# The last feed-forward of a three-layer block: the second tile's down product one turn later, and a score product of the attention one block earlier

## The reference

```python
def conv_ffn(h, w_up, conv_w, conv_b, w_down):
    a, g = jnp.split(h @ w_up, 2, axis=-1)
    return (a * jax.nn.gelu(dwconv_centred(g, conv_w, conv_b), approximate=False)) @ w_down
```

## Time and profile before

| | before |
|---|---|
| median of three runs | 1090.57 us (1090.29 to 1094.52) |
| the profiled execution | 1090.13 us |
| its span, first to last instruction | 1088.3 us |
| TensorE matmul busy | 1060.3 us |
| VectorE, ScalarE busy | 791.5 us, 548.8 us |
| mean granted TensorE clock | 0.994 of full |
| DMA traffic | 232.91 MB |

### The profile page before, as it was taken

One profiled execution on the slowest core, in us unless ns is written; L12 is line 12 of the kernel. 1 busy time (PEld: TensorE's weight loads), 2 busy tenths in 40 slices (PEclk: granted clock), 3 DMA queues, 4 the chain that ended last, 5 costly groups with the idle time before them and its releaser, 6 DMA issues. The chain is left out here.

```text
span 1088.3 us, 20414 instructions
## 1 busy us (share of the span) xinstructions
PE 1060.3 (97%) x8020; PEld 966.8 (89%) x8020; DVE 791.5 (73%) x1374; ACT 548.8 (50%) x934; POOL 112.0 (10%) x133
## 2 busy tenths in 40 slices
PE   6999999999999999999999999999999998999998
PEld 1889778999999989888999999888866898999998
DVE  2688785787888778846677775797349767777776
ACT  4642485544444474655444444446347664444442
POOL 2102004000000027510000000300330010000000
PEclk9999999999999999999999999999999999999999
DMA  9981375698988716475787785396630144545541
GB/s 363 411 316 42 114 242 166 259 351 325 354 324 337 288 59 243 164 268 203 268 284 270 265 290 199 106 326 203 134 78 28 40 156 155 193 162 195 169 169 39
DMA packets 68594, 232.91 MB, mean 214 GB/s; under 512 B 12144, under 2 KB 12432, under 8 KB 68144
## 3 DMA queue, kind: packets, MB, share of 16 engines
q1 hardware_dynamic: 62496, 227.27, 58.9%
q0 software_dynamic: 5888, 3.73, 1.6%
q10 hardware_dynamic: 144, 1.05, 0.3%
HBM read 230.91 MB, written 1.05 MB: 213 GB/s over the span
## 5 line engine op out<-in xcount | busy, mean ns | idle before, releaser
L1757 PE MATMUL bank<-h_hi,w_hi 128*128 128x256 f32 (+2 forms) x1424 | 409.4, 288 | 4.7 <-DVE h_lo L1709 1.7
L1759 PE MATMUL bank<-h_hi,w_lo 128*128 128x256 f32 (+2 forms) x1424 | 406.0, 285 | 0.0
L1758 PE MATMUL bank<-h_lo,w_hi 128*128 128x256 f32 (+2 forms) x1424 | 405.3, 285 | 0.0
L1114 DVE TENSOR_TENSOR w_lo<-w_raw,w_hi 128x1024 fp32r<-128x1024 f32 x271 | 328.5, 1233 | 71.8 <-ACT w_hi L674 70.5
L674 ACT CAST w_hi<-w_raw 128x1024 fp32r<-128x1024 f32 x271 | 276.5, 1046 | 79.8 <-PE bank L1759 70.3
L1757 PEld LDWEIGHTS bank<-h_hi,w_hi 128*128 128x128 f32 x1424 | 269.4, 189 | 13.8 <-issue 7.3
L1758 PEld LDWEIGHTS bank<-h_lo,w_hi 128*128 128x128 f32 x1424 | 269.8, 189 | 1.6 <-issue 0.2
L1759 PEld LDWEIGHTS bank<-h_hi,w_lo 128*128 128x128 f32 x1424 | 269.8, 189 | 1.4
L1757 PE MATMUL bank<-g_hi,w_hi 128*128 128x256 f32 x544 | 155.4, 286 | 4.2 <-DVE g_lo L1374 2.5
L1758 PE MATMUL bank<-g_lo,w_hi 128*128 128x256 f32 x544 | 153.8, 283 | 0.0
L1759 PE MATMUL bank<-g_hi,w_lo 128*128 128x256 f32 x544 | 153.6, 282 | 0.0
(11 more groups left out here) (181 smaller groups left out, 1243.2 us busy)
## 6 DMA issues: line engine op xcount, KB each, us to landing
w_raw<-weights SPq DMA_DIRECT2D x281, 512.0 KB, 4.9
a_raw<-ada SPq DMA_DIRECT2D x140, 512.0 KB, 5.4
vals<-ada SPq DMA_DIRECT2D x4, 512.0 KB, 8.7
a_raw<-rpb POOLq DMA_DIRECT2D x9, 224.0 KB, 16.8
bias<-rpb POOLq DMA_DIRECT2D x7, 224.0 KB, 8.4
xT<-xt SPq DMA_DIRECT2D x1, 1024.0 KB, 9.4
big<-ctx SPq DMA_DIRECT2D x1, 1024.0 KB, 14.1
big<-ctx ACTq DMA_DIRECT2D x1, 1024.0 KB, 6.5
```

The source lines that it names most:

```text
L1114: nc.vector.tensor_tensor(w_lo[:, s, :], w_raw[:, s, :], w_hi[:, s, :].bitcast(fp), SUB)\
L1757: nc.tensor.matmul(out, a_hi, b_hi, start=start, stop=False)
L1758: nc.tensor.matmul(out, a_hi, b_lo, start=False, stop=False)
L1759: return nc.tensor.matmul(out, a_lo, b_hi, start=False, stop=stop)
```

## The change

In the last feed-forward `down(1)` of turn t is taken out of turn t and done in turn t + 1, between `up(0)` and `up(1)` (`down_before`). Turn 0 has five blocks, turns 1 to 10 have six, and turn 10 does its own `down(1)` at the end besides. The weights lie in memory in that order, so the splits of turn i are of blocks 3 to 8 counted from its start instead of 4 to 9. The sixth block (`W_FF2 + 5`) is split ahead of the feed-forward by both engines: by ScalarE before the root of norm 7, by VectorE before the inverse. `hi(6)` and `lo(6)` fall away in turn 0 and are there in turn 10. The waits of `normed` on `w_used` are counted anew.

In the attention, score pair 1 stands before value block 23 instead of after it, and the wait for the last turned queries stands before score pair 2.

```diff
@@ ScalarE, before the root of norm 7; VectorE, before invert(("norm", 7))
-                    split_to(W_FF2 + LEAD)
+                    split_to(W_FF2 + 5)
@@ ScalarE and VectorE, hi(j) and lo(j) of ffn
+                        if layer == 2:
+                            j -= 1
...
-                    hi(5)
+                    hi(5, layer < 2 or i)
...
-                    hi(6, splits_on)
+                    hi(6, splits_on and (layer < 2 or i) or layer == 2 and i == FT // 2 - 1)
@@ VectorE, normed
-                        dve.wait_ge(w_used, 6 * i + (w0 + 2 * s + e + 1))
+                        dve.wait_ge(w_used, 6 * i + (w0 + 3 * s + e + (first and s == 0)))
@@ VectorE, turn
-                    lo(5)
+                    lo(5, layer < 2 or not first)
...
-                    lo(6, splits_on)
+                    lo(6, splits_on and not (layer == 2 and first) or layer == 2 and final)
@@ TensorE, attention
-                        if name == "mla" and j == 0:
-                            pe.wait_ge(head_ready, MLA_H)
+                        if j == 0:
+                            pe.wait_ge(head_ready, MLA_H if name == "mla" else MLA_H + UNITS)
@@ TensorE, ffn
+                    def down_before():
+                        pe.wait_ge(split_done, 6 * i + splits_to(w0 + 1))
+                        pe.wait_ge(ff_lo, 2 * i + g0)
+                        for j in range(KT):
+                            a = wtile(w0 + 1, j * P, P)
+                            ins = split3(bank[tiles[("acc", layer, j // 2)][0]][:, (j % 2) * T:(j % 2 + 1) * T], a[0], a[1],
+                                         g_hi[:, 1, :], g_lo[:, 1, :], False, False)
+                        ins.then_inc(w_used, 1)
...
                     up(0)
+                    if layer == 2 and not (isinstance(i, int) and i == 0):
+                        down_before()
                     up(1)
                     last = isinstance(i, int) and i == FT // 2 - 1
-                    for s in range(2):
+                    for s in range(2 if layer < 2 or last else 1):
@@ TensorE, values of the attention
-                if s == 22:
+                if s >= 22:
                     pe.wait_ge(head_ready, MLA_H + 10)
-                    scores("na", head_rows, 0)
+                    scores("na", head_rows, s - 22)
...
-            pe.wait_ge(head_ready, MLA_H + UNITS)
-            attention("na", NA_H, 16, head_rows, lambda h, kt: vals[:, kt, h * NA_D:(h + 1) * NA_D], 12, 1)
+            attention("na", NA_H, 16, head_rows, lambda h, kt: vals[:, kt, h * NA_D:(h + 1) * NA_D], 12, 2)
@@ pack_weights
+        if at == W_FF2:
+            n = np.arange(3 * FT).reshape(FT // 2, 6)
+            order = [n[0, :5]] + [np.r_[n[t, 0:2], n[t - 1, 5], n[t, 2:5]] for t in range(1, FT // 2)] + [n[-1, 5:]]
+            w[at:at + 3 * FT] = w[at:at + 3 * FT][np.concatenate(order)]
```

More of the change, by code:

```diff
@@ L1329, in turn @@
                 def turn(i, splits_on=True, more=True):
+                    first, final = (isinstance(i, int) and i == n for n in (0, FT // 2 - 1))
                     def lo(j, on=True):
+                        if layer == 2:
+                            j -= 1
                         if on:
@@ L1381, in turn @@
                         norm_gain(5)
-                    lo(4, layer < 2 or not isinstance(i, int) or i)
-                    lo(5)
+                    lo(4, layer < 2 or not first)
+                    lo(5, layer < 2 or not first)
                     if sums > 1:
@@ L1997, in up @@
                         ws = [w0 + 2 * s + e for e in range(2)]
+                        if layer == 2 and not (isinstance(i, int) and i == 0):
+                            ws = [w0 - 1 + 3 * s + e for e in range(2)]
                         if layer == 2:
```

## The result

The changed kernel took 1085.47 us, the median of five runs (1082.91 to 1086.01). The kernel before, beside it, took 1093.55 (1090.29 to 1094.52): a ratio of 0.9923, interval 0.9897 to 0.9949. With more runs on another chip it was 1084.89 against 1093.81, a ratio of 0.9908 (0.9885 to 0.9931). So it is faster by 8 to 9 us. The forecast was 1081.0, range 1079.0 to 1084.7: the measured time lies 0.8 us above the range. The first profiles show neither plainly. Their spans are 1088.3 and 1083.7 us, 4.6 apart.

The account below looks back on a forecast made before the run. TensorE, busy for 97% of the span, was taken as the bound; 1.25 + 2.63 + 1.56 + 2.8 + 1.0 = 9.2 us off 1090.13 gives 1080.9, put at 1081.0, range 1079 to 1084.7.

Parts of the forecast that it names:

- the level: Whole kernel: 9.2 us off the profiled 1090.13 gives 1080.9; the runs' median is 0.44 higher, so 1081.0.
- The rule of the Trainium skill: Clock gate: slow matmuls differ from run to run; turn 0's half clock might be luck, the sum 1.56 us smaller.
- Turn 0 and the turns after it: Last feed-forward: turn 0 gains 1.25 us at `down(0)`, 2.63 at `down(1)`, 1.56 by the clock; turns 1 to 9, 2.8.
- The price of the clock: Half-clock stretch after turn 0's pauses, expected not to come once they are gone: 1.56 us gained.
- The account of turn 0: Turn 0's chain to `down(0)` is late behind two VectorE splits; with both gone from there, `down(0)` gains 1.25 us.
- The cover of a steady turn: Steady turn: `convolve(0)` starts 2.2 us late, its chain ends at 10.9, wanted at 14.4: 3.5 us in hand.
- Rival C: VectorE falls behind, `down(0)` stalls in all ten turns: 1096; chance 0.04 including the bank rule beside it.
- The attention: Start of the attention: second waiting transpose at 810.0 instead of 811.05, 1.0 us gained; bounds 1.7 and nothing.
- A: Half clock comes elsewhere, or `down(0)` of turn 0 still waits up to 1.3 us: 1082.4 to 1083.7; chance 0.14.
- B: Turn 0 is not mended, its loss having another cause; 2.8 + 1.0 us are left: 1086.3; chance 0.09.
- D: The moved product waits for something new in order, say its block's split; 3.9 us in hand; counted within B.
- the swing of the clock beside C: Going round PSUM banks idles TensorE between groups, the clock swings: 1.56 us a turn, net 1097; 1 in 100.

Follow-up runs that it names:

- fillers in turn 0: Kernel before with two filler matmuls on TensorE between `down(0)` and `down(1)` of turn 0: 1093.51 us against 1093.58, ratio 0.9994.
- the early split alone: Kernel before with the sixth block split ahead of the feed-forward and nothing moved: 1090.62 us against 1093.58, ratio 0.9971.
- changed and timed: The changed kernel once more, timed beside the kernel before in more rounds; its trace took 798.8 us to score pair 0 and 286.0 from there.
- three added operations: Changed kernel with three more split-sized VectorE operations ahead of the first gate tile in turns 1 to 10: feed-forward 238.47 us, period 19.62.

## Why the prediction was wrong in its number and right in most of its steps

**The step that failed is the last one, the level.** I set the sum against one execution of 1090.13 us and put the median 0.44 above it. The four times in view were 1090.13, 1090.29, 1090.57 and 1094.52, and I took the last for a stray. With 24 runs the kernel before has a median of 1093.58 (1088.03 to 1096.89): 1090.13 was a quick execution. Its trace has none of the costly stretches near 186, 398 and 472 us and a mean granted clock of 0.994; of the 24 runs the five at 0.994 or more took 1088.0 to 1092.4 us, the eight at 0.989 or less 1093.4 to 1096.9. 1093.6 less 9.2 is 1084.4; with that step mended the number would have been a microsecond off. The range had room for errors in the gain and none for the level, which alone spreads by several microseconds.

**The rule of the Trainium skill** was weighed in the prediction only against turn 0's stretch, and that was the wrong place for it. At turn 0 the stretch came in each of the three traces that keep the old feed-forward whole, with 12 slow matmuls in one and 15 and 16 in the others, and its removal paid 1.5 us. At the places of the unchanged part, which the prediction didn't look at, it comes in some traces and not in others. The page TensorE: Matmul & The Clock Gate (part 1, on the HAM clock gate) has the number of slow matmuls change from run to run of one kernel. The traces agree.

**Turn 0 and the turns after it**: forecast 1.25 + 2.63 + 1.56 + 2.8 = 8.24 us, measured 8.5. `down(0)` 1.25; the two down products of turn 0 took 10.00 us before and 5.68 now, 4.32 (forecast 4.19; I left out the first matmul after a wait, after which the next starts 0.20 us on instead of 0.12); nine turns at 0.32. The price of the clock, 1.56 in the forecast, was 1.58 against the kernel with fillers in turn 0.

**The account of turn 0** was right in naming the splits ahead of the chain. It gave the whole gain to the change as one; the early split alone carries 3.55 us of it.

**The cover of a steady turn** held, but with less in hand than I wrote. `g_lo` of s = 0 was forecast for 10.9 in the turn and ended at 10.8, the tile of s = 1 for 17.4 and 17.3; these positions were good. The 3.5 us derived from them was not: it is 1.0. Rival C would have begun there already, and its chance was drawn too small for the reason given. That this did no harm here is the luck of a margin that was a third of what I thought.

**The attention**: forecast 1.0 us. It arrived (1.06 us at the first weighing) and half of it was given back: from there to the output projection TensorE needs 48.5 us instead of 48.0, in three steps of 0.15 to 0.19, each at the second transpose of a pair; only the last, at 835.25, has a listed wait, for ScalarE's copy. What holds the other two stays open. The bound "nothing if the later stretch swallows it" was named; the term should have been 0.5 and not 1.0. Rivals A, B and D didn't come. Nor did the swing of the clock beside C: the changed kernel goes from up blocks to down blocks every 8.6 us with 0.12 from matmul to matmul, and no trace of it has a stretch below full clock in the feed-forward.

## What to carry to other kernels

Compare two traces from the last point that the change can't touch, and price the change there; take the level of the whole from many runs, with its spread in the range. The time in hand of an engine whose work repeats is the pause in its loop that waits for the bound engine; handovers inside its own chain and the distance to a tile's use are not to be counted. Test it with added work and read the period of that engine, not only of the bound one: a lag of 0.10 us a turn shows nowhere else until the cover is used up. Before work is moved to cover a late chain, look at what stands ahead of the chain on the same engine: here one early split brought 40% of the gain.

## What had not been expected of the hardware

The same place is followed by a stretch at the 1.2 GHz level in some executions and not in others: without fillers near 472 us in three of 12 traces (changed; changed and timed; fillers in turn 0), near 398 in eight of 12. One costs 1.5 to 1.6 us where TensorE is the bound, and next to nothing where a wait stands right behind it (near 45 us) or where VectorE sets the pace (three added operations). Single runs of the kernel before, whose TensorE is busy for 97% of the span, spread by 9 us (1088.0 to 1096.9), as much as this change is worth.
